# In the expert layer of a decoder step, each pair of row gathers is issued in the other order

## The reference, cut to what matters

```python
q = (c @ w_q).reshape(n, PEER_HEADS, 2, PEER_QDIM // 2)
s = jnp.einsum('nhpd,hpkd->nhpk', q, sub_keys)
s1, i1 = lax.top_k(s[:, :, 0], PEER_TOPK)
s2, i2 = lax.top_k(s[:, :, 1], PEER_TOPK)
...
g = jax.nn.softmax(top, axis=-1)
hid = jax.nn.gelu(jnp.einsum('nd,nhkd->nhk', c, u_tab[experts]), approximate=False)
return jnp.einsum('nhk,nhkd->nd', g * hid, v_tab[experts])
```

## Time and profile before

| | us |
|---|---|
| median of 3 runs | 2654.8 (2649.76 to 2655.9) |
| the profiled execution's own time | 2644.37 |
| its span, first to last instruction | 2642.8 |
| PE busy | 2122.9 (80%) |
| DVE busy | 1124.5 (43%) |
| POOL busy | 851.4 (32%) |
| ACT busy | 376.3 (14%) |
| mean granted TensorE clock | 0.939 |

### The profile page before, as it was taken

One profiled execution on the slowest core, in us unless ns is written; L12 is line 12 of the kernel. 1 busy time (PEld: TensorE's weight loads), 2 busy tenths in 40 slices (PEclk: granted clock), 3 DMA queues, 4 the chain that ended last, 5 costly groups with the idle time before them and its releaser, 6 DMA issues.

```text
span 2642.8 us, 27962 instructions
## 1 busy us (share of the span) xinstructions
PE 2122.9 (80%) x9886; PEld 1222.3 (46%) x9886; DVE 1124.5 (43%) x2194; ACT 376.3 (14%) x788; POOL 851.4 (32%) x598
## 2 busy tenths in 40 slices
PE   8996899899798899777777777777777776776797
PEld 5775566555487676522222232223222222222566
DVE  2000001100175315785676766756655464443412
ACT  2000101001343001201111111111111101101111
POOL 0000000000000002664655655545655575553310
PEclk9998999999866899999999999998999999998998
DMA  4347989997411334999999999998999999999971
GB/s 160 141 156 281 362 345 368 357 363 265 181 71 42 134 132 190 421 417 405 410 409 410 402 406 407 402 409 365 410 413 420 416 417 419 412 422 421 404 305 69
DMA packets 139861, 854.83 MB, mean 323 GB/s; under 512 B 16385, under 2 KB 17218, under 8 KB 54258
## 3 DMA queue, kind: packets, MB, share of 16 engines
q0 software_dynamic: 85248, 612.41, 56.7%
q1 hardware_dynamic: 53938, 238.80, 23.5%
q10 hardware_dynamic: 576, 2.36, 0.2%
HBM read 844.07 MB, written 9.44 MB: 323 GB/s over the span
## 4 chain that ended last, share of the span: by engine, by line
PE 39%; DMA 27%; POOL 10%; issue 10%; DVE 7%; ACT 3%; SPq 3%; POOLq 0%; DVEq 0%; ACTq 0%
PE ps L759 12%; DMA aT<-in_vt,big 11%; DMA wring<-in_vt,big 10%; POOL big L476 6%; PE ps L852 6%; PE ps L1130 6%; PE ps L1155 4%; DMA big<-in_vt,big 3%; DVE big L1495 3%; POOL wring L484 2%; PE ps L868 2%; PE ps L805 2%; POOL aT L484 2%; DMA subk<-in_v 1%; ACT L638 1%
## 5 line engine op out<-in xcount | busy, mean ns | idle before, releaser
L1495 DVE CUSTOM_DVE_ANT_0 big<-big 128x2048 f32<-128x2048 f32 x288 | 660.3, 2293 | 203.1 <-DMA big<-in_u,big 173.7
L476 POOL DMA_INDIRECT big<-in_u,big x288 | 448.2, 1556 | 626.8 <-DVE big L1495 345.2
L1130 PE MATMUL ps<-aT,wring 128*128 128x512 f32 x816 | 383.0, 614 | 142.2 <-DMA aT<-in_vt,big 142.2
L1130 PE MATMUL ps<-wring 128*128 128x512 f32 x816 | 381.7, 612 | 125.8 <-DMA wring<-in_vt,big 125.8
L1130 PEld LDWEIGHTS ps<-aT,wring 128*128 128x128 f32 x816 | 150.4, 194 | 374.8 <-issue 241.9
L1130 PEld LDWEIGHTS ps<-wring 128*128 128x128 f32 x816 | 150.4, 193 | 355.4 <-issue 235.9
L1130 PE MATMUL ps<-big,wring 128*128 128x512 f32 x416 | 205.7, 641 | 88.0 <-DMA big<-in_vt,big 88.0
L446 POOL DMA_DIRECT2D big<-in_s x8 | 4.6, 571 | 726.4 <-PE ps L881 706.7
L671 ACT ACTIVATE wring<-ident,big 128x128 f32<-128x128 f32 x256 | 99.5, 398 | 924.8 <-PE ps L1130 924.8
L852 PE MATMUL ps<-aT,wring 128*128 128x288 f32 x768 | 202.3, 418 | 1.4 <-ACT big L545 1.4
L484 POOL DMA_INDIRECT wring<-in_vt,big x116 | 155.7, 1342 | 114.8 <-PE ps L1146 43.6
(11 more groups left out here) (303 smaller groups left out, 1988.9 us busy)
## 6 DMA issues: line engine op xcount, KB each, us to landing
big<-in_kT SPq DMA_DIRECT2D x128, 512.0 KB, 6.2
wring<-in_w_in SPq DMA_DIRECT2D x48, 1024.0 KB, 6.4
big<-in_v SPq DMA_DIRECT2D x48, 512.0 KB, 6.5
wring<-in_v SPq DMA_DIRECT2D x32, 512.0 KB, 5.4
states<-in_v SPq DMA_DIRECT2D x32, 512.0 KB, 5.8
wring<-in_w_out SPq DMA_DIRECT2D x16, 1024.0 KB, 4.8
big<-in_w_ple SPq DMA_DIRECT2D x9, 1024.0 KB, 26.5
subk<-in_v SPq DMA_DIRECT2D x16, 512.0 KB, 6.7
```

Source lines behind the costliest of these rows:

```text
L476: pool.indirect_dma_start(uring[j % UR], None, A["u"], bass.IndirectOffsetOnAxis(ap=eidx[:, j:j + 1], axis=0)).then_inc(u_in[j % UR], 16)
L1130: mm = pe.matmul(ps[:, 4 * t + c, :], diag[:, j % 4, :], vring2[j % VR][:, c * 512:(c + 1) * 512], start=(j % P == 0), stop=(j % P == P - ...
L1495: dve.tensor_tensor_reduce(prod, uring[j % UR], cnat[:, tile_of(j), :], 1.0, 0.0, ALU.mult, ALU.add, hid[:, j:j + 1]).then_inc(u_read, 1)
```

## The change

In each pair the gather from the second table is issued first, and the one from the first table behind it. Nothing is added or taken away: the same 576 gathers are made, with the same waits and into the same buffers.

```diff
@@ -491,9 +491,9 @@
                     pool.wait_ge(query_mm, NPQ)
                 if j == 3:
                     pool.wait_ge(cn_mm, 12)
+                gather_v(j)
                 if j + LAG < NU:
                     gather_u(j + LAG)
-                gather_v(j)
```

## The result

The change made the kernel 1.3% faster: the median fell from 2652.3 us (4 runs, 2647.9 to 2655.9) to 2617.9 us (4 runs, 2614.3 to 2618.7), a ratio of 0.987 with a 95% interval of 0.985 to 0.989. The forecast was 2619. The profiled execution took 2614.3 us. Its span is 2612.7 us, 30.1 less than before.

The account below looks back on a forecast made before the run. The prediction took the gathers to be bound by transfer, kept below 421 GB/s by a ring of waits that stalls POOL. Saving 30 us in the stream and 6 in the tail, 2654.8 - 36 gave 2619 us, range 2604 to 2632.

Parts of the forecast that it names:

- The stall and the ring: POOL stalls on DVE, 329.4 us in 24 waits; v landing, PE, diagonal, exponential, dot, u, next v form a cycle.
- The gather ahead of the stall: v119 would go out ahead of u139, over 14 us earlier, leaving one more gather queued when POOL is released.
- The lap: Eight units: 9.5 us plus ten gathers (eight after) plus those queued, at 2.49 us; 38.1 us before, 35.6 after, transfer floor 39.8.
- The sum of the stream: Gathers from 1100 us on: shortfall against 421 GB/s is 38.7 us at most, 0 at least; 30 taken.
- the two deep dips: Rate drops at 1780 and 1830 us, too deep for one gather; of 8.7 us together, 3.7 left unrecovered.
- The wait that changes places: u now waits behind v for PE, 4.98 us later; DVE's 12.8 us exponential wait covers it, cost nothing.
- The tail: From 2460 us: v267 moves up two places, third gate tile starts 10.9 us earlier; bounds 0 and 11, 6 taken.
- under 4 us: Sign that the forecast is right: PE's wait for v267, 8.88 us before, falls below 4 us.
- A: Rival: the transfer has no idle to give, 409 GB/s is already what memory gives; no change, 2655 us; chance 0.08.
- B: Rival: POOL hardly outruns the transfer, so half the stream's gain and none at the end; 2640 us; chance 0.17.
- C: Rival: u comes late, DVE's cover under 4.98 us, seven second-tile laps grow; slower, 2690 us; chance 0.04.
- D: Rival: order makes no difference, since v's buffer becomes free only when u's would; 2655 us; chance 0.03.

Follow-up runs that it names:

- the early exponential: Kernel before, gathers in old order, but ACT's exponential put ahead of the last two diagonals of its turn: 2619.6 us, ratio 0.988.
- the two halves: Against the kernel before, v first only in the one pair in eight whose u DVE holds: 2617.9 us; v first in all other pairs only: 2615.4 us.
- a lead of 14: Kernel before with u gathers running 14 units ahead of v instead of 20, order inside a pair unchanged: 2627.7 us, ratio 0.991.

## Why the prediction was right

**The stall and the ring.** The view that a lap is bound by a ring rather than by the 1.00 of the DMA share is borne out by the early exponential, which reaches 421 GB/s with the gathers in their old order. The place was right too: POOL is held at u, with v behind it.

**The gather ahead of the stall.** It does go out ahead, at 1679.14, while u139 waits until 1687.59. But as a cause it is not needed: all other pairs swapped, and this one not, give the same time. The sentence that the extra gather fills the queue mixed up two things; the queue is fuller because the ring has slack.

**The lap.** "Ten gathers before, eight with the change" was the right count, and the change is a lead cut by one. The formula was too low: it gave 38.1 us before, below the floor of 39.8, and left 3 us of a lap to the poor rate. Read strictly it said that the ring was no bound already. The runs give the size: 45.7 us a lap with twelve gathers, 41.5 with ten, and at eight no more than the 40.4 that all other short rings show as well. A line of 2.1 us a gather through the first two would give 37.3 at eight; with 2.49 us a gather it is 36.5. Either is under the floor, as is 39.4 or 39.0 at nine, which is why half of the swaps is enough. I had this formula and still wrote "half of the gain" for nine gathers in what I expected of the two halves. The gain is a step down to a floor, not a share.

**The sum of the stream.** 38.7 us were the bound and 30 the choice; 27.8 came by the rates and 28.1 by the dots. Of the 8.3 us left, 4.3 are in the stretch from 1700 to 1900, near the 3.7 that I had set aside for the two deep dips. That stretch reached 412 GB/s and not the 417 that I had named as a sign.

**The wait that changes places.** POOL's wait for PE at `aT` doubled and u came later, at no cost, as said: DVE's wait for the exponential fell from 12.8 to 10.3 us each and was not used up.

**The tail.** 4.2 us where I took 6. The step that was off is that v267 moves up two places. It moved up one: it was issued 20.5 us behind dot 276 instead of 24.2 and landed 43.9 behind it instead of 48.1. Only u287 changed sides with it; v263 goes out inside the stall, but its rows still have to come ahead of v267. The sign "under 4 us" for PE's wait did not come either, since the spacing of v266 and v267 is the same in both orders. Stream and tail together gave 32.3 us in the profiles, where I had 36.

**The total.** That 2619 and 2617.9 lie 1 us apart is partly luck. By the medians the change saved 34.4 us, 1.6 less than the 36 forecast, and the median of the kernel before, with a fourth run, is 2652.3, 2.5 below the 2654.8 that I started from. The two profiled executions differ by 30.1 us.

**The rivals.** A, no idle to give, is refuted by the rates, 419 to 421 GB/s over hundreds of us. The Trainium skill, "DMA: Bandwidth & Descriptors", section "Where 436 GB/s comes from", puts the limit between HBM and SBUF at about 358 GB/s for a core, as the half of a stack. By it nothing could have been gained; the traces disagree, with 409 before and 419 after from 1100 to 1700 us. Only one core ran here, and whether the limit holds with both at work no run shows. B did not come; 419 is not half of the way. C has its mechanism, late u rows, but neither its place nor its threshold: with DVE's cover at 0.9 us in all the laps held, and what a lead of 14 loses it loses in the tail. D is refuted by v119, 8.5 us ahead.

What stays open is why the laps stop at 40.2 to 40.5 us and not at 39.8, sixteen times 2.49. In the first tile the rates of 418 to 421 account for at most 0.3 us of it, and the change of tile at unit 136 for another 0.1 with the change.

## What to carry to other kernels

A DMA share of 1.00 is no proof that the transfer alone is the bound: here it stood beside 409 GB/s, where 421 could be had. Compare the GB/s of the stretch with the best stretch of the same kind, and look at the time to landing of the first transfer behind a stall. If it is near the shortest in the trace, the queue may run dry because a ring of waits is longer than the transfer. Here every edit that took a place out of the ring, in the order of the transfers or on ACT, gave the same gain, and only down to the floor. A lead of prefetch that is too long can be what closes the ring, since the gather that waits for its buffer holds up the one with the shorter lead behind it.

## What the runs showed of the hardware

A gather instruction on POOL mostly takes 0.94 us while DVE waits or does small work and 2.14 us beside the dots, where one goes out every 2.44 us, at the pace of the dots. That is just below the 2.49 us in which the transfer takes a gather at 421 GB/s, so the queue hardly fills while the dots run. Why the instruction is longer there no run shows. A lead longer by one unit than in the kernel before costs 4%, which I had not expected from a kernel whose DMA share read 1.00.
